# Cumulative sums of an attention's log weights: one fp32 product replaced by two products of split values

## The chip, the core and the metric

The kernel is one program on one core of a Trainium2 chip. The metric is the device time of one execution in microseconds, as the median of several runs. Beside it stands one profiled execution, whose trace has the start and the duration of every instruction on each engine: TensorE (PE, with its weight loads as PEld), VectorE (DVE), ScalarE (ACT), GpSimd (POOL) and the DMA queue of SyncE (SPq). All times below are in microseconds from the first instruction of that execution unless marked ns.

## The reference, cut to what matters

Two transformer blocks run one after the other on 256 tokens of 1024 features. The change is in the second block, in one of its three branches, a stick-breaking attention with 8 heads of 64 features:

```python
z = jnp.einsum("bhqd,bhkd->bhqk", q_blk, k[:, :, :ctx]) * scale
mask = k_pos[None, :] < q_pos[:, None]
log_1m_beta = jnp.where(mask, jax.nn.log_sigmoid(-z), 0.0)
cs = lax.cumsum(log_1m_beta, axis=3)
log_a = jax.nn.log_sigmoid(z) + (cs[..., -1:] - cs)
a = jnp.where(mask, jnp.exp(log_a), 0.0)
outs.append(jnp.einsum("bhqk,bhkd->bhqd", a, v[:, :, :ctx]))
```

The rest of the block around it is an input projection to 6656 columns, a gated spatial mixing (branch a), a 31-tap causal convolution (branch b), sigmoid gates for the three branches, an output projection, and a convolved feed-forward.

## The kernel before

Every large weight goes through the same line. SyncE loads a unit of up to 128x2048 values into one of four `raw` slots. ScalarE copies it to `w_hi` in the type fp32r (`high`, L516). VectorE writes `w_lo = raw - w_hi`, also fp32r (`low`, L866). TensorE then makes three fp32r products for each tile of it: high by high, high by low, low by high (L1361 to L1363). ScalarE and VectorE do this three blocks ahead of TensorE (`AHEAD`), and TensorE waits for `raw_used` of the block before it starts on it.

The stage with the change is `z_in`, the input projection: 26 blocks in the order of `Z_ORDER` (step s is block s). Every engine runs its own loop over the steps, in program order, and meets the others at semaphores. Into these steps the work on the branches is set by hand: `QK_STEP(p)` = 13 + 2p is where the scores of head pair p are made, `U_STEP(p)` = 15 + 2p where their log weights are, `AV_STEP(p)` = 17 + 2p where the values are weighted, for p = 0 to 3. `VLN_STEP` is 13, `SG_STEP` 14, `CV_MEAN_STEP` 22, `CV_VAR_STEP` 23.

For one pair of heads (keys on the partitions, 384 columns of queries a head) the attention goes like this. TensorE makes the scores in two PSUM banks (`scores`, L1666 and L1668). ScalarE computes log(1 + exp(-|z|)) in three passes into `sp_t` (`softplus_log`, L725 to L727). VectorE adds max(z, 0), which gives the softplus `sp` (`softplus`, L1194). GpSimd zeroes what the mask excludes (`mask`, L495). TensorE adds to the scores the product of a triangle of -1 (`neg_upper`) or a square of -1 (`neg_ones`) with `sp`: that is the cumulative sum over the keys (`log_weights`, L1677 to L1681; six fp32 products for a pair, of 256, 128 and 128 columns for each of two heads). VectorE clamps the result into `att` (`clamp`, L1203), ScalarE takes its exponential (`weights`, L731), GpSimd masks again, and TensorE multiplies by the values (`att_values`, L1695 and L1696).

Between these stand, on VectorE, the taps of the convolution (`conv`, L1186; a few in each step by the table `CONV_AT`), and at step 14 the eviction of the spatial mixing to `sgo` and its split to `br_a_hi` and `br_a_lo` (L1244 to L951). The spatial mixing has the PSUM bank pair 6 and 7, which the scores of pair 1 use next; so TensorE's `scores(1)` waits for `br_a` to reach 4, the last of these splits. `log_weights(p)` waits for `sp_masked`, the mask. The column means of the convolution (`cv_mean`, L1753, step 22) wait for the last of the 124 taps (`conv_step`).

Of the kernel before, what the change touches and what calls it, by code (L numbers as in the profile page):

```python
# [20 lines left out]
P = 128  # L21
T = 256
# [50 lines left out]
N_CONST = 10  # L73
# [3 lines left out]
VLN_STEP, SG_STEP = 13, 14  # L77
QK_STEP = lambda p: 13 + 2 * p
# [48 lines left out]
def build_program(nc, x_in, params, ada, ada_half, w, wm_t, sg_bias, sg_ln, out):  # L127
    f32, f32r = mybir.dt.float32, mybir.dt.float32r
    ALU, ACT = mybir.AluOpType, mybir.ActivationFunctionType
    ADD, SUB, MUL, MAX = ALU.add, ALU.subtract, ALU.mult, ALU.max  # L130
    ctx = ExitStack()
    with ctx:
        def sb(name, shape, dt=f32, c=ctx):
            return c.enter_context(nc.sbuf_tensor(name, shape, dt))

        def sem(name):
            return ctx.enter_context(nc.semaphore(name))
# [49 lines left out]
        with ExitStack() as c:  # L187
            br = {}
            for name in ("a", "c"):
                br[name] = [sb(f"br_{name}_{part}", [P, 4, T], f32r, c=c) for part in ("hi", "lo")]  # L190
            cacc = sb("cacc", [P, 4, T], c=c)
            vv = sb("vv", [P, 2, SG], c=c)
            head_ones = sb("head_ones", [P, P], c=c)
            neg_upper = sb("neg_upper", [P, P], c=c)
            neg_ones = sb("neg_ones", [P, P], c=c)
            bn = sb("bn", [P, 2, 8], c=c)
            vstd = sb("vstd", [P, 4], c=c)
            with ExitStack() as early:
                sig = sb("sig", [P, 2, T], c=early)
                sb("unused_gates_head", [P, 4, T], c=early)  # L200
                sgo = sb("sgo", [P, 4, T], c=early)
                vg = sb("vg", [P, 2, SG], c=early)
                wm = sb("wm", [P, HEADS, P], c=early)
                sgb = sb("sgb", [P, 4, P], c=early)
                sgln = sb("sgln", [P, 2, SG], c=early)
            gates = sb("gates", [P, 24, T], c=c)
            with ExitStack() as early:
                cpad = sb("cpad", [P, 4, T + CV_TAPS - 1], c=early)
                sp_t = sb("sp_t", [P, 2, 384], c=early)
            br["b"] = [sb(f"br_b_{part}", [P, 4, T], f32r, c=c) for part in ("hi", "lo")]  # L210
            with ExitStack() as late:
                mg_t = sb("mg_t", [P, 3, T], c=late)
            sp = sb("sp", [P, 2, 512], c=c)
            with ExitStack() as early:
                u_sb = sb("u_sb", [P, 4, T], c=early)
            att = sb("att", [P, 2, 512], c=c)
# [8 lines left out]
        ps = ctx.enter_context(nc.psum_tensor("ps", [P, 8, 2 * T], f32))  # L225
# [15 lines left out]
        const_set = sem("const_set")  # L241
# [61 lines left out]
        sp_log = sem("sp_log")  # L303
        sp_ready = sem("sp_ready")
        sp_masked = sem("sp_masked")
        loga_done = sem("loga_done")
        loga_low = sem("loga_low")
        att_exp = sem("att_exp")
# [198 lines left out]
        def _(act):  # L507
            e = act
# [210 lines left out]
            def softplus_log(p):  # L719
# [6 lines left out]
                ch.link(e.activation(sp_t[:, :, :], sp_t[:, :, :], ACT.Exp, scale=-1.0))  # L726
                e.activation(sp_t[:, :, :], sp_t[:, :, :], ACT.Ln, bias=1.0).then_inc(sp_log, 1)  # L727

            def weights(p):
                e.wait_ge(loga_low, p + 1)  # L730
                e.activation(att[:, :, 0:384], att[:, :, 0:384], ACT.Exp).then_inc(att_exp, 1)  # L731

            for s, kind in enumerate(Z_ORDER):
                g = FIRST["z_in"] + s
                high_at(g + AHEAD)
                bank = Z_FILL[s] % 2 if s in Z_FILL else None
                if s == CV_VAR_STEP:
                    for t in range(2):
                        e.wait_ge(cv_cent, 2 * t + 2)
                        square(SQ["cv"] + t, flat(cacc[:, 2 * t:2 * t + 2, :]))  # L740
# [117 lines left out]
        def _(dve):  # L858
# [329 lines left out]
            def softplus(p):  # L1188

                e.wait_ge(sp_log, p + 1)  # L1190
                if p:
# [2 lines left out]
                e.scalar_tensor_tensor(sp[:, :, 0:384], ps[:, zb:zb + 2, 0:384], 0.0, sp_t[:, :, :], MAX, ADD)\  # L1194
                 .then_inc(sp_ready, 1)

            def clamp(p):

                e.wait_ge(loga_done, p + 1)
                if p:  # L1200
                    e.wait_ge(att_done, p)
                zb = Z_BANKS[p % 2]
                e.tensor_scalar(att[:, :, 0:384], ps[:, zb:zb + 2, 0:384], 0.0, None, ALU.min).then_inc(loga_low, 1)  # L1203
# [4 lines left out]

            for s, kind in enumerate(Z_ORDER):
                g = FIRST["z_in"] + s  # L1210
                if s != SG_STEP:
                    ahead_at(g + AHEAD)
                bank = Z_FILL[s] % 2 if s in Z_FILL else None
# [141 lines left out]
        def _(pe):  # L1355
# [316 lines left out]
            def log_weights(p):  # L1672

                zb = Z_BANKS[p % 2]
                e.wait_ge(sp_masked, p + 1)
                for h in range(2):
                    e.matmul(ps[:, zb + h, 0:T], neg_upper[:, :], sp[:, h, 0:T], start=False, stop=True,  # L1677
                             skip_group_check=True)
                    e.matmul(ps[:, zb + h, P:T], neg_ones[:, :], sp[:, h, T:T + P], start=False, stop=True,
                             skip_group_check=True)  # L1680
                    mm = e.matmul(ps[:, zb + h, T:T + P], neg_upper[:, :], sp[:, h, T:T + P], start=False, stop=True,  # L1681
                                  skip_group_check=True)
                mm.then_inc(loga_done, 1)

            def att_values(p):
# [211 lines left out]
```

## Time and profile before

| | |
|---|---|
| runs | 766.95, 766.12, 766.15 us; median 766.15 us |
| profiled execution | 766.32 us, of which 764.6 us are the span from the first to the last instruction |
| PE busy | 749.6 us (98% of the span) |
| PEld busy | 696.9 us (91%) |
| DVE busy | 545.1 us (71%) |
| ACT busy | 360.3 us (47%) |
| POOL busy | 10.7 us (1%) |
| mean granted clock of TensorE | 0.998 of 2.4 GHz |

TensorE is busy nearly all the time; the other engines have gaps. The shares are means over nine stages. A matmul's duration in the trace is longer than what it takes of the engine's time, since matmuls overlap: what one costs is read from the distance between starts. One fp32 matmul of the program shows as two matmul records, one fp32r matmul as one.

### The profile page before, as it was taken

Reading aid. Unit: us, or ns where it says so; the run is one execution under the profiler, and the core shown is the slowest. Engines: PE = TensorE matmul, PEld = TensorE weight load, DVE = VectorE, ACT = ScalarE, POOL = GpSimd, SP = SyncE. Lnnn points to the kernel's source line nnn. Section 1 sums busy time; section 2 is a strip of 40 time slices with the busy share of each in tenths; the row PEclk is TensorE's granted clock in tenths of the full one; section 3 lists DMA queues with packets and bytes.
Section 4 is the critical chain, followed back from the end, with each engine's and each line's share of the span. In section 5 each row is a group of like instructions: output and inputs, shape, how many; then the busy total and the mean of one; then the engine's idle time right before and its main releaser. Section 6 shows DMA issues by size and latency. Waiting matters only on the chain.

```text
span 764.6 us, 13287 instructions
## 1 busy us (share of the span) xinstructions
PE 749.6 (98%) x5388; PEld 696.9 (91%) x5388; DVE 545.1 (71%) x770; ACT 360.3 (47%) x442; POOL 10.7 (1%) x27
## 2 busy tenths in 40 slices
PE   6999999999999999999999999999989999999998
PEld 5789955999998888899979999999989999999998
DVE  5677988856566743458899967769757888888441
ACT  4116332754553333475555366484546455554330
POOL 0000000000000000020000001000000000000000
PEclk9999999999999999999999999999999999999999
DMA  9999998364566964436445342437543544533640
GB/s 272 303 335 386 385 355 322 129 222 165 175 209 219 346 205 165 166 124 221 165 165 171 113 159 97 166 110 250 205 165 123 207 167 174 192 116 124 216 142 28
DMA packets 61728, 152.18 MB, mean 199 GB/s; under 512 B 2992, under 2 KB 42288, under 8 KB 51440
## 3 DMA queue, kind: packets, MB, share of 16 engines
q1 hardware_dynamic: 61312, 150.20, 57.3%
q0 software_dynamic: 368, 1.31, 0.5%
q8 instruction: 34, 0.56, 0.3%
q14 instruction: 14, 0.11, 0.0%
HBM read 150.45 MB, written 1.05 MB: 198 GB/s over the span
## 4 chain that ended last, share of the span: by engine, by line
PE 95%; SPq 3%; DMA 1%; ACT 1%; DVE 0%; issue 0%; DVEq 0%
PE ps L1363 21%; PE ps L1361 21%; PE ps L1362 21%; PE ps L1438 4%; PE ps L1518 4%; PE ps L1517 4%; PE ps L1516 4%; PE ps L1563 4%; SPq L390 2%; DMA keyed_odd<-in_w_sc_in 1%; PE ps L1652 1%; PE ps L1651 1%; PE ps L1650 1%; PE ps L1378 1%; PE ps L1501 1%; PE ps L1503 1%
## 5 line engine op out<-in xcount | busy, mean ns | idle before, releaser
L866 DVE TENSOR_TENSOR w_lo<-raw,w_hi 128x2048 fp32r<-128x2048 f32 (+2 forms) x116 | 246.2, 2124 | 94.2 <-ACT w_hi L516 93.9
L1361 PE MATMUL ps<-a_hi,w_hi 128*128 128x256 f32 x1072 | 305.2, 285 | 0.0
L1363 PE MATMUL ps<-a_hi,w_lo 128*128 128x256 f32 x1072 | 303.5, 283 | 0.0
L1362 PE MATMUL ps<-a_lo,w_hi 128*128 128x256 f32 x1072 | 301.1, 281 | 0.0
L516 ACT ACTIVATE w_hi<-raw 128x2048 fp32r<-128x2048 f32 (+2 forms) x116 | 205.8, 1778 | 105.5 <-PE ps L1518 50.3
L1362 PEld LDWEIGHTS ps<-a_lo,w_hi 128*128 128x128 f32 x1072 | 203.5, 190 | 0.6 <-issue 0.5
L1361 PEld LDWEIGHTS ps<-a_hi,w_hi 128*128 128x128 f32 x1072 | 201.7, 188 | 1.3 <-issue 0.6
L1363 PEld LDWEIGHTS ps<-a_hi,w_lo 128*128 128x128 f32 x1072 | 200.8, 187 | 0.0
L1516 PE MATMUL ps<-w_hi,hid_hi 128*128 128x512 f32 x128 | 50.9, 398 | 0.0
L1518 PE MATMUL ps<-w_hi,hid_lo 128*128 128x512 f32 x128 | 50.8, 397 | 0.0
L1517 PE MATMUL ps<-w_lo,hid_hi 128*128 128x512 f32 x128 | 50.8, 397 | 0.0
L842 ACT ACTIVATE up_u<-ps,par 128x256 f32<-128x256 f32 x44 | 22.5, 561 | 58.7 <-PE ps L1363 55.7
L1363 PE MATMUL ps<-up_hi,w_lo 128*128 128x256 f32 x176 | 49.8, 283 | 0.0
L1361 PE MATMUL ps<-up_hi,w_hi 128*128 128x256 f32 x176 | 49.8, 283 | 0.0
L1324 DVE SCALAR_TENSOR_TENSOR up_u<-ps,par,up_u 128x255 f32<-128x255 f32 (+1 forms) x88 | 38.4, 478 | 15.6 <-ACT up_u L842 13.4
L1362 PE MATMUL ps<-up_lo,w_hi 128*128 128x256 f32 x176 | 49.4, 280 | 0.0
L1186 DVE SCALAR_TENSOR_TENSOR cacc<-cpad,par,cacc 128x256 f32<-128x256 f32 x120 | 49.2, 480 | 0.0
L1362 PEld LDWEIGHTS ps<-up_lo,w_hi 128*128 128x128 f32 x176 | 33.5, 190 | 0.0
L1361 PEld LDWEIGHTS ps<-up_hi,w_hi 128*128 128x128 f32 x176 | 33.0, 188 | 0.0
L1363 PEld LDWEIGHTS ps<-up_hi,w_lo 128*128 128x128 f32 x176 | 33.0, 187 | 0.0
L1518 PEld LDWEIGHTS ps<-w_hi,hid_lo 128*128 128x128 f32 x128 | 24.1, 188 | 5.8
L1516 PEld LDWEIGHTS ps<-w_hi,hid_hi 128*128 128x128 f32 x128 | 24.1, 189 | 5.7
(242 smaller groups left out, 914.1 us busy)
## 6 DMA issues: line engine op xcount, KB each, us to landing
raw<-in_w_z_in SPq DMA_DIRECT2D x26, 1024.0 KB, 4.7
raw<-in_w_up SPq DMA_DIRECT2D x22, 1024.0 KB, 4.8
raw<-in_w_mlp_in SPq DMA_DIRECT2D x16, 1024.0 KB, 4.8
raw<-in_w_mlp_out SPq DMA_DIRECT2D x16, 1024.0 KB, 5.6
raw<-in_w_down SPq DMA_DIRECT2D x16, 704.0 KB, 4.1
raw<-in_ada SPq DMA_DIRECT2D x32, 256.0 KB, 6.2
raw<-in_ada_half SPq DMA_DIRECT2D x8, 1024.0 KB, 7.4
raw<-in_ada SPq DMA_DIRECT2D x8, 1024.0 KB, 7.1
```

The costliest lines, as they stand in the source:

```text
L516: e.activation(w_hi[:, slot, 0:words], raw[:, unit_slot, 0:words], ACT.Copy).then_inc(w_high, 1)
L866: e.tensor_tensor(w_lo[:, slot, 0:words], raw[:, unit_slot, 0:words], w_hi[:, slot, 0:words].bitcast(f32), SUB).then_inc(raw_used, 1)
L1186: e.scalar_tensor_tensor(cacc[:, i, :], src, wt, cacc[:, i, :], MUL, ADD).then_inc(conv_step, 1)
L1324: ins = e.scalar_tensor_tensor(dst, ps[:, b, h * T:(h + 1) * T - o], pdyn("up_w", it * 24 + (3 * (2 * b + h) + tap)), dst, MUL, ADD)
L1361: e.matmul(dst, w_hi[:, slot, cols], hi, start=start, stop=False, skip_group_check=skip)
L1362: e.matmul(dst, w_hi[:, slot, cols], lo, start=False, stop=False, skip_group_check=skip)
L1363: return e.matmul(dst, w_lo[:, slot, cols], hi, start=False, stop=stop, skip_group_check=skip)
L1438: mm = e.matmul(half(bank, h), lhs, y[:, k, :], start=opens, stop=k == DT - 1, skip_group_check=True)
L1516: e.matmul(dst, hi[:, tok], high_w, start=first, stop=False)
L1517: e.matmul(dst, hi[:, tok], low_w, start=False, stop=False)
L1518: return e.matmul(dst, lo[:, tok], high_w, start=False, stop=final)
L1563: mm = e.matmul(ps[:, 2 * c + h, :].rearrange("p (n q) -> p n q", n=4), sc_y[:, k, c * P:(c + 1) * P], by_feature[:, 4 * h:4 * h + 4, k, : ...
```

## The change

The softplus values are split, as the weights are: ScalarE copies masked `sp` to `sp_hi` in fp32r (`log_high`), VectorE writes `sp_lo = sp - sp_hi` in fp32r (`log_low`), both at the head of step `QK_STEP(p) + 1`. The two sign matrices are copied once to fp32r (`ones_r`, `upper_r`; -1 and 0 need no low part). `log_weights` then makes twelve fp32r products in place of six fp32 ones, and waits for `sp_low` in place of `sp_masked`. The fp32 sign matrices move into unused columns of `sp`; the new buffers lie where early ones have ended.

```diff
-            neg_upper = sb("neg_upper", [P, P], c=c)
-            neg_ones = sb("neg_ones", [P, P], c=c)
...
-                sb("unused_gates_head", [P, 4, T], c=early)
+                sb("unused_gates_head", [P, 3, T], c=early)
...
+                upper_r = sb("upper_r", [P, P], f32r, c=early)
+                ones_r = sb("ones_r", [P, P], f32r, c=early)
...
-                sp_t = sb("sp_t", [P, 2, 384], c=early)
+                with ExitStack() as log_part:
+                    sp_t = sb("sp_t", [P, 2, 384], c=log_part)
+                sp_hi = sb("sp_hi", [P, 2, 384], f32r, c=early)
...
             sp = sb("sp", [P, 2, 512], c=c)
+            neg_ones, neg_upper = sp[:, 0, 384:512], sp[:, 1, 384:512]
+            sp_lo = sb("sp_lo", [P, 2, 384], f32r, c=c)
...
+            def log_high(p):
+
+                e.wait_ge(sp_masked, p + 1)
+                if p:
+                    e.wait_ge(loga_done, p)
+                e.activation(sp_hi[:, :, :], sp[:, :, 0:384], ACT.Copy).then_inc(sp_high, 1)
...
                 high_at(g + AHEAD)
                 bank = Z_FILL[s] % 2 if s in Z_FILL else None
+                if s == VLN_STEP:
+                    e.wait_ge(const_set, N_CONST)
+                    e.activation(ones_r[:, :], neg_ones[:, :], ACT.Copy).then_inc(sign_ready, 1)
+                    e.activation(upper_r[:, :], neg_upper[:, :], ACT.Copy).then_inc(sign_ready, 1)
+                for p in range(4):
+                    if s == QK_STEP(p) + 1:
+                        log_high(p)
...
+            def log_low(p):
+
+                e.wait_ge(sp_high, p + 1)
+                e.tensor_tensor(sp_lo[:, :, :], sp[:, :, 0:384], sp_hi[:, :, :].bitcast(f32), SUB).then_inc(sp_low, 1)
...
                 g = FIRST["z_in"] + s
+                for p in range(4):
+                    if s == QK_STEP(p) + 1:
+                        log_low(p)
                 if s != SG_STEP:
                     ahead_at(g + AHEAD)
...
             def log_weights(p):
 
                 zb = Z_BANKS[p % 2]
-                e.wait_ge(sp_masked, p + 1)
-                for h in range(2):
-                    e.matmul(ps[:, zb + h, 0:T], neg_upper[:, :], sp[:, h, 0:T], start=False, stop=True,
-                             skip_group_check=True)
...
+                e.wait_ge(sign_ready, 2)
+                e.wait_ge(sp_low, p + 1)
+                for part in (sp_hi, sp_lo):
+                    for h in range(2):
+                        e.matmul(ps[:, zb + h, 0:T], upper_r[:, :], part[:, h, 0:T], start=False, stop=True,
+                                 skip_group_check=True)
+                        e.matmul(ps[:, zb + h, P:T], ones_r[:, :], part[:, h, T:T + P], start=False, stop=True,
+                                 skip_group_check=True)
+                        mm = e.matmul(ps[:, zb + h, T:T + P], upper_r[:, :], part[:, h, T:T + P], start=False, stop=True,
+                                      skip_group_check=True)
                 mm.then_inc(loga_done, 1)
```

Where the two new operations stand in their engines' order is best seen in the list of instructions. First VectorE in the kernel before, from the softplus of pair 0 (end of step 13) to the first eviction of step 14, whose last split is what `br_a` counts:

```order
L1186 SCALAR_TENSOR_TENSOR cacc<-cpad,par,cacc 128x256 [waits conv_step] x4
L1194 SCALAR_TENSOR_TENSOR sp<-ps,sp_t 128x2x384 [waits sp_log]
L1244 TENSOR_TENSOR sgo<-ps,sgb 128x128 [waits z_free_act,sg_done]
L1244 TENSOR_TENSOR sgo<-ps,sgb 128x128
L1248 TENSOR_TENSOR sgo<-sgo,u_sb 128x256 [waits dve_self]
L950 CAST br_a_hi<-sgo 128x256 [waits dve_self]
L951 TENSOR_TENSOR br_a_lo<-sgo,br_a_hi 128x256 [waits dve_self]
```

And the same place in the changed kernel:

```order
L1207 SCALAR_TENSOR_TENSOR cacc<-cpad,par,cacc 128x256 [waits conv_step] x4
L1215 SCALAR_TENSOR_TENSOR sp<-ps,sp_t 128x2x384 [waits sp_log]
L1221 TENSOR_TENSOR sp_lo<-sp,sp_hi 128x768 [waits sp_high]
L1273 TENSOR_TENSOR sgo<-ps,sgb 128x128 [waits z_free_act,sg_done]
L1273 TENSOR_TENSOR sgo<-ps,sgb 128x128
L1277 TENSOR_TENSOR sgo<-sgo,u_sb 128x256 [waits dve_self]
L971 CAST br_a_hi<-sgo 128x256 [waits dve_self]
```

The subtraction stands directly behind the softplus whose masked copy it needs, and ahead of all of step 14. For pairs 1 to 3 it stands the same way, directly behind the softplus, and ahead of the weights' low part and of the taps of its step.

ScalarE in the changed kernel, from the last pass of pair 0 (step 13) to step 15; before, the same rows stood there without the `sp_hi` one:

```order
L734 ACTIVATE sp_t<-sp_t 128x768 [waits act_self]
L523 ACTIVATE w_hi<-raw 128x2048 [waits w_used,raw_in1]
L741 ACTIVATE sp_hi<-sp 128x768 [waits sp_masked]
L803 ACTIVATE gates<-ps,par 128x256 [waits w_used]
L803 ACTIVATE gates<-ps,par 128x256
L523 ACTIVATE w_hi<-raw 128x2048 [waits w_used,raw_in2]
```

The copy to `sp_hi` comes behind a weight's copy and ahead of the gates. The copies of the sign matrices stand in step 13, between a weight's copy and `u_sb`.

## Rows read from the trace of the kernel before

**Rows 1.** The page's first part: busy time, share, instructions.

```profile
PE 749.6 (98%) x5388; PEld 696.9 (91%) x5388; DVE 545.1 (71%) x770; ACT 360.3 (47%) x442; POOL 10.7 (1%) x27
```

**Rows 2.** Windows: stretch, length, then each engine's busy time, granted clock.

```profile
405.00:500.00 95.00, 95.00 (x780) 90.95 (x780) 77.67 (x132) 52.03 (x67) 5.10 (x8) 1.00 0.38 133
```

**Rows 3.** Timeline of PE: start, union of durations, instructions with their record count.

```profile
431.23 0.59 PE L1677 MATMUL ps<-sp,neg_upper 128*128 128x256 f32 x2
431.66 0.39 PE L1679 MATMUL ps<-sp,neg_ones 128*128 128x128 f32 x2
431.89 0.39 PE L1681 MATMUL ps<-sp,neg_upper 128*128 128x128 f32 x2
...
433.08 0.71 PE L1666 MATMUL ps<-y 64*128 64x256 f32 x4
...
446.45 0.70 PE L1677 MATMUL ps<-sp,neg_upper 128*128 128x256 f32 x2
...
448.41 0.71 PE L1666 MATMUL ps<-y 64*128 64x256 f32 x4
...
477.12 0.70 PE L1677 MATMUL ps<-sp,neg_upper 128*128 128x256 f32 x2
...
484.74 1.89 PE L1753 MATMUL ps<-cacc,ones 128*128 128x256 f32 x8
```

**Rows 4.** Timeline of DVE: start, duration; in brackets the idle time before.

```profile
424.93 0.95 DVE L1194 SCALAR_TENSOR_TENSOR sp<-ps,sp_t 128x768 f32<-128x768 f32 x1
425.80 0.48 DVE L1244 TENSOR_TENSOR sgo<-ps,sgb 128x128 f32<-128x128 f32 x2
...
432.23 0.42 DVE L951 TENSOR_TENSOR br_a_lo<-sgo,br_a_hi 128x256 fp32r<-128x256 f32 x1
...
444.07 0.96 DVE L1194 SCALAR_TENSOR_TENSOR sp<-ps,sp_t 128x768 f32<-128x768 f32 x1 [3.37 <-ACT sp_t L727]
445.87 2.29 DVE L866 TENSOR_TENSOR w_lo<-raw,w_hi 128x2048 fp32r<-128x2048 f32 x1 [0.84 <-ACT w_hi L516]
...
481.65 2.07 DVE L1186 SCALAR_TENSOR_TENSOR cacc<-cpad,par,cacc 128x256 f32<-128x256 f32 x5
```

**Rows 5.** Timeline of POOL, the masks of `sp` for pairs 0, 1, 3.

```profile
426.01 0.64 POOL L495 TENSOR_SCALAR_AFFINE_SELECT sp<-sp 128x512 f32<-128x512 f32 x1 [92.80 <-DVE sp L1194]
...
445.16 0.64 POOL L495 TENSOR_SCALAR_AFFINE_SELECT sp<-sp 128x512 f32<-128x512 f32 x1 [2.82 <-DVE sp L1194]
...
474.54 0.64 POOL L495 TENSOR_SCALAR_AFFINE_SELECT sp<-sp 128x512 f32<-128x512 f32 x1 [2.81 <-DVE sp L1194]
```

**Rows 6.** Timeline of ACT.

```profile
416.76 0.60 ACT L767 ACTIVATE u_sb<-ps 128x512 f32<-128x512 f32 x1 [3.36 <-PE ps L1363]
...
443.19 0.85 ACT L727 ACTIVATE sp_t<-sp_t 128x768 f32<-128x768 f32 x1
443.94 1.90 ACT L516 ACTIVATE w_hi<-raw 128x2048 fp32r<-128x2048 f32 x1
```

**Rows 7.** Timeline of PE: two fp32r products of 256 columns, neighbours.

```profile
434.28 0.28 PE L1363 MATMUL ps<-a_hi,w_lo 128*128 128x256 f32 x1
434.40 0.28 PE L1361 MATMUL ps<-a_hi,w_hi 128*128 128x256 f32 x1
```

**Rows 8.** The weight loads of one line whose products have one column.

```profile
L1419 PEld LDWEIGHTS ps<-silu_c,raw x16: 191/192/193, 11.7 to 13.4; 128*128 128x128 f32 x16
```

**Rows 9.** Groups by line from 405 to 500, weight loads: busy, mean ns.

```profile
L1362 PEld LDWEIGHTS ps<-a_lo,w_hi 128*128 128x128 f32 x207 | 39.1, 189 | 0.1
...
L1677 PEld LDWEIGHTS ps<-sp,neg_upper 128*128 128x128 f32 x16 | 2.4, 190 | 0.5 <-issue 0.5
```

**Rows 10.** Timeline of PE behind its longest wait in the up stage.

```profile
570.14 0.55 PE L1501 MATMUL ps<-a_hi,w_hi 128*128 128x256 f32 x1 [2.14 <-ACT a_hi L561]
```

**Rows 11.** Windows around that wait; the third number from the end is the clock.

```profile
566.20:569.90 3.70, 1.16 (x5) 0.68 (x4) 0.84 (x3) 1.83 (x4) 0.00 (x0) 1.00 0.31 131
569.90:573.30 3.40, 3.16 (x15) 3.19 (x16) 3.40 (x11) 3.40 (x9) 0.00 (x0) 0.50 0.00 0
```

More of the change, by code:

```diff
@@ L305, in build_program @@
         sp_masked = sem("sp_masked")
+        sign_ready = sem("sign_ready")
+        sp_high = sem("sp_high")
+        sp_low = sem("sp_low")
         loga_done = sem("loga_done")
@@ L1674, in log_weights @@
                 zb = Z_BANKS[p % 2]
-                e.wait_ge(sp_masked, p + 1)
-                for h in range(2):
-                    e.matmul(ps[:, zb + h, 0:T], neg_upper[:, :], sp[:, h, 0:T], start=False, stop=True,
-                             skip_group_check=True)
[L1679 to L1682, printed above, removed]
+                e.wait_ge(sign_ready, 2)
[8 more added lines that the diff above has]
+                                      skip_group_check=True)
                 mm.then_inc(loga_done, 1)
```

## The prediction

> **What bounds the kernel now.** I read the page's first part, then windows, then the timelines of the engines between 405 and 500 us, where all four head pairs lie. TensorE is busy 98% of the span [rows 1], and in the stage of the change 95.00 of 95.00 us, at full granted clock [rows 2]. So TensorE sets the end, and two things can move it: what its own instructions cost, and a wait that did not exist. The second needs the distance between a result and its use, which no share shows. I looked for it in three places.
>
> First place, `scores(1)`. TensorE starts it at 433.08, right behind `log_weights(0)` [rows 3]. It waits for the last split of branch a, which ends at 432.23 + 0.42 = 432.65 [rows 4]. Room: 0.43 us.
>
> Second place, `log_weights(p)`. For pair 1 the mask ends at 445.16 + 0.64 = 445.80 [rows 5], TensorE uses it at 446.45 [rows 3]: 0.65 us of room. For pair 3 it is 475.18 against 477.12: 1.94 us. For pair 0 it is 426.65 against 431.23.
>
> Third place, `cv_mean`, at 484.74 [rows 3]. The last taps end at 481.65 + 2.07 = 483.72 [rows 4]: 1.02 us of room.
>
> VectorE has idle time, but little that it could give away here. Before the softplus of a pair it waits for ScalarE's passes [rows 4], those wait for the previous pair's exponential, that for VectorE's clamp. It is a ring: clamp, exponential, three passes, softplus, weights and taps, next clamp. What is put into the ring makes each turn longer, and nothing in it waits for TensorE.
>
> **The change, part by part.**
>
> *TensorE's products.* For pair 0 the six fp32 products and the switch to the scores take 433.08 - 431.23 = 1.85 us: 0.43 for 256 columns, 0.23 for 128 (431.66 to 431.89) [rows 3]. For pair 1 it is 448.41 - 446.45 = 1.96; the 0.11 more stands behind `att_values`. An fp32r product of 256 columns takes 0.12 [rows 7]. One of 128 columns with 128 columns of weights isn't in the trace. Lower bound: half of 0.12, 0.06. Next row: sixteen fp32 records of one moving column start from 11.7 to 13.4, 0.113 each, so the weight load holds the distance there [rows 8]. Upper bound: the fp32 price, 0.23, if the short form gains nothing. I take 0.113, since a weight load in fp32r lasts 189 ns and in fp32 190 [rows 9]. Twelve products are then 4 x 0.12 + 8 x 0.113 = 1.38, against 2 x 0.43 + 4 x 0.225 = 1.76: 0.38 less for a pair (0.8 less at the lower bound, 0.56 more at the upper).
>
> The Trainium skill (TensorE: Matmul & The Clock Gate, Weight-path perf modes) says that a fast weight load is on when there are 128 weights and the input type is not FP32. If fp32r counted as such a type, its load would be shorter than fp32's; the trace has 189 and 190 ns, so it does not agree for this type. By the page the products would go to the lower bound, 0.8 us less for a pair in place of 0.38, and the waits below would swallow it.
>
> *ScalarE, signs.* Two copies of 128x128 in step 13, ahead of `u_sb`, before which ScalarE waits 3.36 us [rows 6]. Each costs less than the 0.60 of the four times wider `u_sb`. Hidden. Without that cover they would cost under 1.2 us, once.
>
> *ScalarE and VectorE, pair 0.* Now the copy waits for the mask (426.65), takes 0.85 like a pass of the same 768 columns [rows 6], and the subtraction takes 0.96 like the softplus of 768 columns [rows 4]. From GpSimd to ScalarE I allow 0.1 (VectorE to GpSimd shows 426.01 - 425.88 = 0.13 [rows 4, 5]), from ScalarE to VectorE 0.03 (444.04 to 444.07 [rows 4, 6]). So: copy 426.75 to 427.6, subtraction 427.63 to 428.6. Next instructions start about 0.1 before the end of the one ahead, so `sgo` starts at 428.5 in place of 425.80: **VectorE is 2.7 us late**. Queued behind the subtraction is the whole of step 14, and who waits for it is TensorE: `br_a` is complete at 435.35, `scores(1)` starts at 435.4 in place of 433.08. TensorE is 2.3 us late, and the 0.38 us of cheaper products has gone into the wait. ScalarE's gates of step 14 are late too; the bank that they free is needed behind `scores(1)`, so after 435.4, and comes at about 428.4.
>
> *Pair 1.* Before, the weight's copy ended at 443.94 + 1.90 = 445.84, and VectorE went on with the low part at 445.87 [rows 4, 6]. Now `sp_hi` follows: 445.9 to 446.75, the subtraction 446.78 to 447.75, the low part at 447.67. **1.8 us more per turn**, all of it serial. With the 2.7 from before, `sp_low` is there at 450.45. TensorE arrives at 446.45 + 2.3 = 448.77 and starts at 450.5: 4.05 late, after a wait of 1.7. Cheaper products give back 0.38 + 0.1 (the switch lies in the wait): 3.6 late.
>
> *Pairs 2 and 3.* Pair 2 goes the same way: VectorE 6.3 us late behind it. For pair 3 the mask ends at 475.18 + 6.3 = 481.48, `sp_low` at 483.4. TensorE would be there at about 481.7 (pair 2 makes it 4.5 late, by the same steps) and starts at 483.45, 6.3 late, 5.85 after the products.
>
> *The mean of the convolution.* VectorE is late by 2.7 + 3 x 1.8 = 8.1, so the taps end at 491.8. TensorE would arrive at 484.74 + 5.85 = 490.6; it starts at 491.87, **7.1 us late**. From here on I count no further wait. The squares for the variance follow VectorE, which is then 8.1 late against TensorE's 7.1; if they had no room for that 1.0, it would come on top. The weights for the blocks are ahead: VectorE's low part is for a block three later, some 17 us of TensorE's work, against at most 8.1 us.
>
> *Sum.* 764.6 + 7.1 = 771.7 for the span. Against the profiled execution's own time that is 766.32 + 7.1 = 773.4; the median of the runs is 0.17 less, so 773.3. The price of the products hardly enters: at the upper bound they are 0.94 us dearer than I took for pair 3, and the wait for the taps holds 1.3.
>
> The bounds of the hand-overs: with nothing from GpSimd to ScalarE, pair 0 gives 2.6 and a turn 1.75 (the weight's copy ends last there), the end 6.8 later. With 0.3 it is 2.9 and 2.0: 7.9 later. If the copy to `sp_hi` costs 0.70 instead of 0.85, 0.6 less; if the subtraction runs 0.2 dearer, 0.8 more.
>
> **The rivals.**
>
> *The products at 0.23 (they don't do what the change says).* They cost 4 x 0.12 + 8 x 0.23 = 2.3 in place of 1.76. By the waits above the end stays at 773.3, at most 773.6. Nothing in the trace speaks against it, since no short fp32r product is in it. Chance 0.33.
>
> *The clock falls in the new waits.* In the up stage TensorE waits 2.14 us, in a window in which it is busy 1.16 of 3.70, and in the 3.40 us after it the granted clock is 0.50 [rows 10, 11]. The new waits are 1.2 to 2.7 us long, but each stands alone in dense work. One fall costs 3.4 x 0.5 = 1.7 us of work. After one of the first waits the next swallows it; after the last ones 0.4 to 1.7 stay. Time: 773.7 to 775.0, I take 774.8. Chance 0.12. The same fall in the up stage could also be missed once everything is shifted: 1.5 less, which is in the range.
>
> *TensorE keeps the pace* (the other side). If the ring had slack enough, only the products would count: 4 x -0.38 = -1.5, so 764.6; at the lower bound of the products 4 x -0.8, so 763.0. It decides if the copy and the subtraction together take less than 0.43 us behind the mask's own 0.64 at step 14 and less than 0.65 for pair 1. By the rows they take 1.8. Chance 0.03; that such slack is there for a part and the sum lands within 0.2%, another 0.02.
>
> The 763.0 is also where the Trainium skill's fast weight load (TensorE: Matmul & The Clock Gate, Weight-path perf modes) would lead if TensorE kept the pace.
>
> **How the numbers follow.** The forecast (waits in the ring, products at 0.113) has 0.50, the rival with the same end 0.33, the clock 0.12, the two others 0.05. Predicted 773.3. The cases that agree on the ring span 772.0 to 774.9 by their bounds; I widen to 771.4 and 775.4 for a clock fall won or lost and for the 1.0 at the squares. What a measurement can tell from no change is about 0.2%, 1.5 us: slower 0.95, same 0.02, faster 0.03.
>
> **What would show it.** In the changed trace: TensorE waits before `scores(1)` for VectorE's last `br_a_lo`, before `log_weights` of pairs 1 to 3 for the subtraction, and before `cv_mean` for the taps, 8.5 us together; a distance of 0.11 or of 0.23 between short products; VectorE idle 1.7 us before the first subtraction. It would be wrong if the ring had room that I missed, if the mask, copy and subtraction overlap, or if the clock falls more than once.

## The result, and the profile after

The changed kernel takes 772.86 us (median of 4 runs, 771.79 to 774.55), the kernel before on the same chip 766.55 us (766.12 to 767.48): a ratio of 1.0084, 95% interval 1.0069 to 1.0100. It is slower, by 6.3 us. The profiled execution took 774.55 us, with a span of 772.8 us.

The page's first part of the changed kernel, to be read against [rows 1]:

```profile
PE 752.4 (97%) x5388; PEld 699.8 (91%) x5388; DVE 548.2 (71%) x774; ACT 364.3 (47%) x448; POOL 10.7 (1%) x27
```

No share moved by more than a point: VectorE has 3.1 us more work, ScalarE 4.0, and TensorE is still at 97%. The loss can't be seen there. The windows can show it. Here is the changed kernel over the stretch of [rows 2], then from the start of `scores(0)` to the start of `cv_mean` (the stage), and from there to the end; the third figure from the end of a row is the granted clock:

```profile
405.00:500.00 95.00, 89.46 (x730) 86.20 (x728) 76.43 (x123) 50.68 (x65) 5.11 (x8) 0.96 0.35 121
...
416.71:491.82 75.11, 69.57 (x569) 66.97 (x569) 58.57 (x93) 38.48 (x49) 4.47 (x7) 0.95 0.34 117
491.82:772.80 280.98, 275.48 (x2250) 273.34 (x2248) 196.65 (x291) 138.90 (x162) 0.64 (x1) 0.99 0.46 158
```

And the same two stretches of the kernel before:

```profile
416.65:484.74 68.09, 68.09 (x569) 65.07 (x569) 55.73 (x90) 35.22 (x46) 4.46 (x7) 1.00 0.37 132
484.74:764.60 279.86, 274.33 (x2250) 272.19 (x2248) 196.26 (x290) 138.77 (x162) 0.64 (x1) 0.99 0.45 158
```

Of the 8.2 us between the two spans, 7.0 lie in the stage, where TensorE was busy throughout and now isn't, 1.1 behind it, and 0.1 ahead. What ends the new idle time is in the list of TensorE's waits of the changed kernel (sum, times, longest):

```profile
PE ps L1708 <- DVE sp_lo L1221: 2.9, 2, 1.7
PE ps L1695 <- DVE br_a_lo L972: 2.5, 1, 2.5
PE ps L1530 <- ACT a_hi L568: 2.1, 1, 2.1
```

The third row was there before [rows 10]; the first two are new, and both are for VectorE. VectorE's timeline of the changed kernel shows why it is late, against [rows 4]:

```profile
424.99 0.95 DVE L1215 SCALAR_TENSOR_TENSOR sp<-ps,sp_t 128x768 f32<-128x768 f32 x1
427.62 0.96 DVE L1221 TENSOR_TENSOR sp_lo<-sp,sp_hi 128x768 fp32r<-128x768 f32 x1 [1.68 <-ACT sp_hi L741]
428.50 0.48 DVE L1273 TENSOR_TENSOR sgo<-ps,sgb 128x128 f32<-128x128 f32 x2
...
434.74 0.43 DVE L972 TENSOR_TENSOR br_a_lo<-sgo,br_a_hi 128x256 fp32r<-128x256 f32 x1
...
446.57 0.96 DVE L1215 SCALAR_TENSOR_TENSOR sp<-ps,sp_t 128x768 f32<-128x768 f32 x1 [3.37 <-ACT sp_t L734]
449.21 0.96 DVE L1221 TENSOR_TENSOR sp_lo<-sp,sp_hi 128x768 fp32r<-128x768 f32 x1 [1.68 <-ACT sp_hi L741]
450.09 2.29 DVE L887 TENSOR_TENSOR w_lo<-raw,w_hi 128x2048 fp32r<-128x2048 f32 x1
...
462.77 0.96 DVE L1215 SCALAR_TENSOR_TENSOR sp<-ps,sp_t 128x768 f32<-128x768 f32 x1 [2.58 <-ACT sp_t L734]
...
489.26 2.06 DVE L1207 SCALAR_TENSOR_TENSOR cacc<-cpad,par,cacc 128x256 f32<-128x256 f32 x5
```

Each subtraction stands behind 1.68 us in which VectorE does nothing, since mask and copy run on other engines in that time; its own 0.96 comes on top. `sgo` begins at 428.50 in place of 425.80, 2.7 later, and the last `br_a_lo` ends at 435.17 in place of 432.65. The last taps end at 491.32 in place of 483.72: VectorE is 7.6 us late. GpSimd's mask and ScalarE's copy in the same trace:

```profile
426.07 0.64 POOL L502 TENSOR_SCALAR_AFFINE_SELECT sp<-sp 128x512 f32<-128x512 f32 x1 [92.70 <-DVE sp L1215]
```
```profile
426.74 0.85 ACT L741 ACTIVATE sp_hi<-sp 128x768 fp32r<-128x768 f32 x1 [2.94 <-POOL sp L502]
...
446.45 1.90 ACT L523 ACTIVATE w_hi<-raw 128x2048 fp32r<-128x2048 f32 x1
448.34 0.84 ACT L741 ACTIVATE sp_hi<-sp 128x768 fp32r<-128x768 f32 x1
```

The mask ends at 426.71, the copy starts at 426.74: 0.03 from GpSimd to ScalarE. For pair 1 the copy follows right at the end of the weight's copy, 448.35. TensorE's timeline of the changed kernel has the products and two of the waits:

```profile
431.58 0.34 PE L1708 MATMUL ps<-sp_hi,upper_r 128*128 128x256 f32 x1
431.76 0.22 PE L1710 MATMUL ps<-sp_hi,ones_r 128*128 128x128 f32 x1
431.81 0.28 PE L1712 MATMUL ps<-sp_hi,upper_r 128*128 128x128 f32 x1
431.93 0.34 PE L1708 MATMUL ps<-sp_lo,upper_r 128*128 128x256 f32 x1
...
435.31 0.71 PE L1695 MATMUL ps<-y 64*128 64x256 f32 x4 [2.53 <-DVE br_a_lo L972]
...
436.47 0.41 PE L1391 MATMUL ps<-a_lo,w_hi 128*128 128x256 f32 x1
436.68 0.41 PE L1392 MATMUL ps<-a_hi,w_lo 128*128 128x256 f32 x1
...
450.32 0.36 PE L1708 MATMUL ps<-sp_hi,upper_r 128*128 128x256 f32 x1
...
483.10 0.36 PE L1708 MATMUL ps<-sp_hi,upper_r 128*128 128x256 f32 x1 [1.67 <-DVE sp_lo L1221]
```

A head's three products for one part take 431.93 - 431.58 = 0.35 us, so twelve take 1.4. The products of 256 columns at 436.47 and 436.68 stand 0.21 apart, where [rows 7] have 0.12: TensorE's clock has fallen behind the first wait. The windows of the changed kernel around the two waits, and in the up stage:

```profile
433.00:436.20 3.20, 0.89 (x9) 0.80 (x9) 3.06 (x8) 0.00 (x0) 0.00 (x0) 1.00 0.00 0
436.20:439.70 3.50, 3.50 (x18) 3.50 (x18) 3.50 (x4) 0.00 (x0) 0.00 (x0) 0.51 0.36 87
480.80:484.00 3.20, 1.53 (x16) 1.23 (x13) 2.00 (x2) 3.20 (x5) 0.29 (x1) 1.00 0.00 0
484.00:487.50 3.50, 3.50 (x18) 3.50 (x18) 3.50 (x7) 1.23 (x3) 0.00 (x0) 0.51 0.33 65
...
576.00:583.00 7.00, 5.79 (x27) 5.82 (x28) 6.87 (x17) 5.02 (x10) 0.00 (x0) 0.52 0.00 0
```

Behind each of these two waits TensorE ran some 3.4 us at the half level, 1.2 GHz (0.51 in the windows of 3.50). In the up stage the half level lasts 7 us here, where the kernel before had 3.4 [rows 11]. Behind the fall at 484.0 the taps, ready at 491.32, were no longer what `cv_mean` waited for: it follows its own predecessors, at 491.82.

### The profile page after: what moved, and what is told of

The parts are those of the page before. It is cut to its first block, busy times and chain, and to the rows that moved or that the text cites. A ratio compares the mean times of both kernels' runs of the same rounds, so it can differ in the third digit from the quotient of the medians.

```text
span 772.8 us, 13304 instructions
## 1 busy us (share of the span) xinstructions
PE 752.4 (97%) x5388; PEld 699.8 (91%) x5388; DVE 548.2 (71%) x774; ACT 364.3 (47%) x448; POOL 10.7 (1%) x27
## 3 DMA queue, kind: packets, MB, share of 16 engines
q0 software_dynamic: 368, 1.31, 0.5%
## 4 chain that ended last, share of the span: by engine, by line
PE 86%; DVE 6%; ACT 3%; SPq 3%; issue 1%; DMA 1%; POOL 0%; DVEq 0%; ACTq 0%; POOLq 0%
PE ps L1392 19%; PE ps L1391 19%; PE ps L1390 19%; PE ps L1467 4%; PE ps L1547 4%; PE ps L1546 4%; PE ps L1545 4%; PE ps L1592 4%; SPq L397 2%; DVE w_lo L887 2%; DVE cacc L1207 2%; DMA keyed_odd<-in_w_sc_in 1%; PE ps L1680 1%; PE ps L1681 1%; PE ps L1679 1%
```

## Experiments

Theory: the loss is VectorE's lateness in the ring, handed to TensorE at `scores(1)`, at `log_weights` and at `cv_mean`; the products themselves gain. Rivals: the products are what costs; the falls of the clock are what costs. Each profile is cut as above, at the start of `scores(0)` and at the start of `cv_mean`. All numbers are us; "half" counts the stretches of about 3.4 us at half clock in the stage and behind it (7 us on end are two). The waits stand in order of time: the first of a row is at `scores(1)`, the next are at `log_weights` of pairs 1 to 3, and "mean" is the one at `cv_mean`.

| kernel | stage | behind it | half | TensorE's waits in the stage |
|---|---|---|---|---|
| before | 68.09 | 279.86 | 0, 1 | none |
| changed | 75.11 | 280.98 | 2, 2 | 2.53, 0.1, 1.28, 1.67 |
| changed, again | 74.63 | 278.57 | 1, 0 | 2.53, 0.14, 1.26, 1.63, mean 0.92 |
| split only | 74.64 | 278.53 | 0, 0 | 2.10, 1.56, 0.83, 1.22, mean 0.53 |
| products only | 67.10 | 280.03 | 0, 1 | 0.09, mean 0.44 |
| low part of pair 0 late | 73.49 | 281.10 | 1, 2 | 0.95, 1.56, 1.26, 1.67 |
| clamp first | 70.47 | 279.70 | 1, 1 | 2.53 |
| waits filled | 74.66 | 280.03 | 0, 1 | 0.16, 1.65, 1.27, 0.05, mean 0.99 |
| before, clamp first | 68.08 | 279.72 | 0, 1 | none |
| low part on GpSimd | 69.51 | 279.73 | 0, 1 | 1.31, 1.75 |
| ring filled | 67.35 | 281.08 | 0, 2 | 0.95 |
| softplus(0) first | 67.50 | 279.97 | 0, 1 | 0.47, 0.58 |
| taps later | 66.88 | 279.96 | 0, 1 | 0.47 |

### The split alone

The changed kernel with the six fp32 products back; it still waits for `sp_low`, whose values it does not use.

```diff
                 e.wait_ge(sp_low, p + 1)
-                for part in (sp_hi, sp_lo):
-                    for h in range(2):
-                        e.matmul(ps[:, zb + h, 0:T], upper_r[:, :], part[:, h, 0:T], start=False, stop=True,
...
+                for h in range(2):
+                    e.matmul(ps[:, zb + h, 0:T], neg_upper[:, :], sp[:, h, 0:T], start=False, stop=True,
```

> Change: the changed kernel with its copy to sp_hi, its subtraction to sp_lo and all its waits, but log_weights makes the six fp32 products of the kernel before. Theory W (the copy and subtraction lengthen the ring of VectorE and ScalarE, and TensorE waits for it): the products lie in front of waits, so the time stays that of the changed kernel within 0.7 us, about 6.4 to 7 above the kernel before; TensorE still waits before scores(1), log_weights of pairs 1 to 3, but less, as it gets there later. Theory P (the short fp32r products themselves are what costs): back to the kernel before, +0. If costs simply add up with products 0.38 cheaper a pair: +7.9.

773.57 us (771.92 to 774.48) against 766.37: 1.0098 (1.0085 to 1.0112). The windows of this kernel, stage and the part behind it:

```profile
416.93:491.57 74.64, 68.41 (x569) 65.04 (x568) 58.10 (x93) 38.48 (x49) 4.48 (x7) 1.00 0.33 115
491.57:770.10 278.53, 273.02 (x2248) 270.87 (x2248) 196.98 (x291) 138.92 (x162) 0.64 (x1) 1.00 0.47 160
```

And its waits:

```profile
PE ps L1707 <- DVE sp_lo L1221: 3.6, 3, 1.6
...
PE ps L1695 <- DVE br_a_lo L972: 2.1, 1, 2.1
...
PE ps L1783 <- DVE cacc L1207: 0.5, 1, 0.5
```

The stage is 6.55 longer than before at full clock throughout, with all five waits: VectorE's lateness alone makes the loss. If costs simply added up, the dearer products would have made the time 7.9 longer; it is 7.2. Dearer products only shorten the waits in front of `cv_mean`, whose start is set by the taps.

### The products alone

The kernel before with twelve fp32r products of the same rounded `sp`. It leaves out the split; the sums come out doubled.

```diff
-            sp = sb("sp", [P, 2, 512], c=c)
+            sp = sb("sp", [P, 2, 512], f32r, c=c)
...
+                for part in (sp, sp):
```

> Change: the kernel before with the sign matrices copied to fp32r and twelve fp32r products, all of them of one tile that the softplus writes as fp32r; there is no split (so high part used twice, the sums are doubled: it leaves out the split) and log_weights waits for the mask as before. Theory W: nothing waits, TensorE sets the pace, 4 x -0.38 and up to 0.1 more for each: -1.5 to -1.9 us against the kernel before. Theory P: +6.

766.01 us (764.44 to 767.09, 11 runs) against 766.37: 0.9997 (0.9987 to 1.0006). The stage is 1.0 shorter, and TensorE's timeline of this kernel shows what stopped it:

```profile
484.57 1.78 PE L1762 MATMUL ps<-cacc,ones 128*128 128x256 f32 x7 [0.44 <-DVE cacc L1193]
```

The products gave at least 1.5 (1.0 and the two waits, 0.53), and 1.7 where the taps hold nothing up (with the ring filled, below: 68.09 + 0.95 - 67.35). The taps had just 1.02 of room, so the rest became a wait. Not even the cheaper products by themselves have their full worth in this order: the forecast of 1.5 to 1.9 was missed.

### The low part of pair 0 behind the first tile of the spatial mixing, and the clamp ahead of the taps

Each is one move on VectorE in the changed kernel. The first:

```diff
-                for p in range(4):
+                for p in range(1, 4):
                     if s == QK_STEP(p) + 1:
                         log_low(p)
...
+                        if t == 0:
+                            log_low(0)
```

> Change: the changed kernel, only pair 0's subtraction moved behind the first of the four tiles of the spatial mixing, so VectorE has work while mask and copy run. Theory W: VectorE's wait of 1.68 us disappears, scores(1) is late by about 0.9 in place of 2.5, and as the ring keeps the whole lead, TensorE's later starts all move 1.7 earlier: 1.7 us below the changed kernel, +4.7 against before. If only the later turns of the ring count (slack takes up pair 0): 0 below the changed kernel. Theory K (clock falls make most of it): below by up to 3, since the longest wait goes.

772.12 us (771.34 to 774.06): 1.0075 (1.0061 to 1.0088). `scores(1)` waits 0.95 in place of 2.53, and the stage is 1.6 shorter, as expected. The three waits for the subtractions are what they are in the changed kernel where no fall goes before them (1.56, 1.26, 1.67; 1.65 and 1.27 with the waits filled). The time is 5.75 above the kernel before, where 4.7 was forecast; the profile had two stretches at half clock behind the stage. The second move:

```diff
-                if s in CONV_AT:
-                    first = sum(n for step, n in CONV_AT.items() if step < s)
-                    conv(first, first + CONV_AT[s])
                 for p in range(4):
...
                         clamp(p)
+                if s in CONV_AT:
+                    first = sum(n for step, n in CONV_AT.items() if step < s)
+                    conv(first, first + CONV_AT[s])
```

> Change: the changed kernel, only that VectorE clamps att ahead of the step's taps and not behind them (steps 15, 17, 19, 21), so the taps fill its wait for ScalarE's passes. Theory W: a turn of the ring gets about 2.06 shorter (16.2 to 14.1), under TensorE's 14.9 for the same stretch; no wait at log_weights 1 to 3 nor at the taps; only the wait at scores(1) stays, 2.3, less 3 x 0.38: +1.2 against before, up to +2.9 if the clock falls behind that wait. If the ring isn't what TensorE waits for: as the changed kernel, +6.4.

769.59 us (768.38 to 771.42): 1.0049 (1.0033 to 1.0064). It takes the taps, some 2 us, out of the chain clamp, exponential, passes, softplus. All waits but the first, 2.53 at `scores(1)`, are gone.

The stage is 2.4 longer than before. The wait gives 2.53 and the cheaper products take 1.7 back, so the fall of the clock behind the wait cost about 1.5. That is less than half of its 3.4 us: a product takes 0.21 there in place of 0.12. The time, 3.2 above the kernel before, is a little over the 2.9 that was expected with a fall. The same move in the kernel before is the control:

> Control: the kernel before, only with the clamp ahead of the taps. Theory W: TensorE waits for nothing there before and after, so the time is that of the kernel before within 0.2 us, and scores(0) to the mean stays 68.1 us. If the shorter ring by itself gave e4 its gain: about -3.

766.57 us (11 runs): 0.9998 (0.9987 to 1.0008), and a stage of 68.08: where TensorE waits for nothing, a shorter ring gives nothing.

### The waits filled

Products that no one uses stand ahead of two waits, so that TensorE is busy in them.

```diff
+            def fill(n):
+                e.wait_ge(rstd_ready, STATN["cv"])
+                for _ in range(n):
+                    e.matmul(ps[:, STAT, 0:P], head_ones[:, :], head_ones[:, :], start=True, stop=True)
...
                 if p == 1:
+                    fill(10)
                     e.wait_ge(br_a, 4)
...
+                if p == 3:
+                    fill(6)
                 e.wait_ge(sp_low, p + 1)
```

> Change: the changed kernel, and TensorE makes ten small fp32 products (128x128, 0.225 us each, into the unused statistics bank, never read) just ahead of its wait in scores(1), and six ahead of the wait in log_weights(3); they lie in waits of 2.5 and 1.7 us. Theory W alone: they cost nothing and give nothing, +6.4 against before. Theory K (in most runs of the changed kernel the granted clock falls behind these waits, and that costs up to about 0.5 us at the mean of the convolution): no fall to 0.50 between 430 and 500 us in the profile, the distance from scores(0) to the mean of the convolution is set by the last taps, 74.7 us in place of 75.1, and the median falls by 0.3 to 0.6 us, more if the phase of the later fall matters.

773.68 us (773.14 to 774.48): 1.0091 (1.0076 to 1.0106). Its windows, the first two where the changed kernel has its first wait and fall, the third over the stage:

```profile
433.00:436.20 3.20, 3.04 (x28) 2.70 (x27) 3.06 (x8) 0.00 (x0) 0.00 (x0) 1.00 0.02 5
436.20:439.70 3.50, 3.50 (x30) 3.50 (x31) 3.50 (x4) 0.00 (x0) 0.00 (x0) 1.00 0.29 70
```
```profile
416.71:491.37 74.66, 70.54 (x602) 67.49 (x601) 58.12 (x93) 38.48 (x49) 4.48 (x7) 1.00 0.32 115
```

The falls in the stage are gone, and the time is no shorter. That speaks against the clock as the cause, and the table says why: with no fall in the stage the taps set its end, at 74.66. The changed kernel once more:

> The changed kernel once more, for a comparison on one chip and for how much of its time is chance. Theory W: +6.4 against before, scores(0) to the mean 74.7 to 75.1 us. Theory K: the spread of its runs is that of the number of clock falls; the run with none behind the waits lies 0.5 us and more below the others.

773.33 us (771.62 to 773.94) against 767.17: 1.0083 (1.0070 to 1.0097). Its stage is 74.63 although the clock fell behind `scores(1)`: the next wait, for `sp_lo` of pair 1, is 0.14 here and 1.65 where nothing fell. So what the fall cost, 1.5 by this difference, went into it. Only the fall behind the last `log_weights`, in the first profile of the changed kernel, came through, with 75.11 - 74.65 = 0.5, the part of its 1.5 that is more than the wait for the taps. Without one at that place the taps held `cv_mean`:

```profile
492.13 1.13 PE L1784 MATMUL ps<-cacc,ones 128*128 128x256 f32 x4 [0.92 <-DVE cacc L1207]
```

### The subtraction on GpSimd

The clamp ahead of the taps, and GpSimd makes `sp_lo` in VectorE's place.

```diff
                 mask(sp, sp_masked, p + 1)
+                e.wait_ge(sp_high, p + 1)
+                e.tensor_tensor(sp_lo[:, :, :], sp[:, :, 0:384], sp_hi[:, :, :].bitcast(f32), SUB).then_inc(sp_low, 1)
```

> Change: the changed kernel with the subtraction to sp_lo made by GpSimd right behind its mask, not by VectorE, and the clamp ahead of the taps. Theory W: VectorE's order has nothing new in it, so scores(1) starts as in the kernel before, without a wait; the copy and a subtraction of 1 to 2.5 us on GpSimd end before log_weights(0) (room 4.6 us) and, as the clamp's move gives 2.06 us per turn, before log_weights of the others. TensorE then keeps the pace: 4 x -0.38 and 3 x -0.1 at most, -1.5 to -1.9 against before, scores(0) to the mean 66.3 us. If GpSimd takes over 3 us or slows VectorE down: a wait at log_weights(1) of 1 us or more.

769.53 us (767.52 to 772.07): 1.0041 (1.0027 to 1.0054), where 1.5 to 1.9 us below the kernel before was forecast: missed. The profiled execution is the fastest of the eight, and no fall is in its stage, which is 1.4 longer than before. Of the runs the two at a mean granted clock of 0.998 took 767.52 and 767.67, the three at 0.993 770.95 to 772.07: in the median falls of the clock are counted along with the waits. The tile `sp_lo` of this kernel (least, median and most ns):

```profile
L510 POOL TENSOR_TENSOR sp_lo<-sp,sp_hi x4: 1848/3022/3057, 427.6 to 474.5; 128x768 fp32r<-128x768 f32 x4
```

Beside it VectorE is slower too, as its timeline shows:

```profile
427.53 0.48 DVE L1267 TENSOR_TENSOR sgo<-ps,sgb 128x128 f32<-128x128 f32 x2
428.05 1.67 DVE L1271 TENSOR_TENSOR sgo<-sgo,u_sb 128x256 f32<-128x256 f32 x1
...
430.93 0.43 DVE L1271 TENSOR_TENSOR sgo<-sgo,u_sb 128x256 f32<-128x256 f32 x1
...
445.03 2.29 DVE L889 TENSOR_TENSOR w_lo<-raw,w_hi 128x2048 fp32r<-128x2048 f32 x1 [0.85 <-ACT w_hi L525]
```

And GpSimd's:

```profile
427.58 1.85 POOL L510 TENSOR_TENSOR sp_lo<-sp,sp_hi 128x768 fp32r<-128x768 f32 x1 [1.03 <-ACT sp_hi L743]
...
445.98 3.00 POOL L510 TENSOR_TENSOR sp_lo<-sp,sp_hi 128x768 fp32r<-128x768 f32 x1 [1.03 <-ACT sp_hi L743]
```

The same instruction takes 0.43 alone and 1.67 while GpSimd subtracts from 427.58 to 429.43. The Trainium skill (SBUF — State Buffer, SBUF: two separate sides) says that a VectorE instruction with two inputs in SBUF and a GpSimd instruction that reads SBUF exclude each other for the whole instruction. The trace agrees: VectorE's instruction is 1.67 - 0.43 = 1.24 longer, GpSimd had 1.38 still to go when it began, and the eviction with one input in PSUM beside it kept its 0.48. It agrees the other way round too: GpSimd's 3.00 of pair 1 began at 445.98, while VectorE's low part, with two inputs in SBUF, ran to 447.32, and it is 1.15 longer than the 1.85 of pair 0. Two waits of TensorE stay: 1.31 at `scores(1)`, which the slowed multiplication by `u_sb` makes, and 1.75 at `log_weights(1)`, which GpSimd's 3 us make.

### The ring filled, and two more orders of it

The subtractions stay on VectorE, but what VectorE waits through is filled: four taps ahead of each of the last three, the first tile of the spatial mixing ahead of pair 0's, and the clamp ahead of the taps.

```diff
+                for p in range(1, 4):
                     if s == QK_STEP(p) + 1:
+                        conv(taps_done(s), taps_done(s) + 4)
                         log_low(p)
...
+                        if t == 0:
+                            log_low(0)
...
+                if s in CONV_AT:
+                    early = 4 if s in (16, 18, 20) else 0
+                    conv(taps_done(s) + early, taps_done(s) + CONV_AT[s])
```

> Change: the changed kernel with its subtraction still on VectorE, but no wait of VectorE left bare: pair 0's behind the first tile of the spatial mixing, the others' behind four taps of their step, and the clamp ahead of the taps. Theory W: a turn of the ring is 12.6 us, TensorE's 14.9; only scores(1) waits, 0.9 us. scores(0) to the mean: 68.1 + 0.6 - 3 x 0.46 = 67.3 us, -0.8 against before. If VectorE's added 0.96 us a turn is by itself what TensorE waits for: +3 or more.

765.97 us (764.08 to 768.02, 11 runs) against 766.4: 0.9989 (0.9977 to 1.0000). The stage came out at the forecast 67.3, the time 0.4 below the kernel before, where 0.8 was forecast. VectorE's timeline of this kernel at pair 1:

```profile
443.86 0.96 DVE L1215 SCALAR_TENSOR_TENSOR sp<-ps,sp_t 128x768 f32<-128x768 f32 x1 [1.01 <-ACT sp_t L734]
444.73 2.04 DVE L1207 SCALAR_TENSOR_TENSOR cacc<-cpad,par,cacc 128x256 f32<-128x256 f32 x4
446.70 0.94 DVE L1224 TENSOR_TENSOR sp_lo<-sp,sp_hi 128x768 fp32r<-128x768 f32 x1
```

The taps stand where the 1.68 us stood, and the subtraction waits for nothing. With the split in place and VectorE's waits filled, the stage is shorter than before the change. This kernel has every copy, subtraction, new buffer and semaphore of the changed one: in this order none of them costs TensorE more than the 0.95 at `scores(1)`, which the products outweigh. Next, `softplus(0)` moves ahead of the taps of step 13, whose number becomes 2, with 4 in step 14:

```diff
-CONV_AT = {**{s: 7 for s in range(2, 8)}, **{s: 8 for s in range(8, 13)}, 13: 4, 14: 2, **{s: 5 for s in range(15, 22)}, 18: 6}
+CONV_AT = {**{s: 7 for s in range(2, 8)}, **{s: 8 for s in range(8, 13)}, 13: 2, 14: 4, **{s: 5 for s in range(15, 22)}, 18: 6}
...
+                if s == QK_STEP(0):
+                    softplus(0)
                 if s in CONV_AT:
```

> Change: e8, and in step 13 the softplus of pair 0 ahead of the taps, two of which move to step 14. Theory W: mask and copy of pair 0 end earlier, and the spatial mixing's eviction starts when TensorE has it ready, 0.3 us earlier than before; scores(1) waits about 0.5 in place of 0.95 us. scores(0) to the mean of the convolution 67.0 us (kernel before 68.1, e8 67.35), time 1.1 us below the kernel before. If scores(1) does not wait for br_a alone: as e8.

766.04 us (764.34 to 767.26, 11 runs) against 767.17: 0.9987 (0.9978 to 0.9996). `scores(1)` waits only 0.47, as expected, but the taps moved to step 14 made VectorE late for pair 1, a new wait of 0.58, and the stage came out at 67.50 in place of 67.0. Last, step 14 keeps its 2 taps and step 16 has 7:

```diff
-CONV_AT = {**{s: 7 for s in range(2, 8)}, **{s: 8 for s in range(8, 13)}, 13: 2, 14: 4, **{s: 5 for s in range(15, 22)}, 18: 6}
+CONV_AT = {**{s: 7 for s in range(2, 8)}, **{s: 8 for s in range(8, 13)}, 13: 2, 14: 2, **{s: 5 for s in range(15, 22)}, 16: 7, 18: 6}
```

> Change: e9, only that two taps lie in step 16 and not in step 14, where they stood between pair 0 and the clamp. Theory W: in e9 they made log_weights(1) wait 0.58 us; moved, VectorE reaches the clamp 0.8 us earlier and that wait goes, scores(1) keeps its 0.47. scores(0) to the mean 66.9 us in place of e9's 67.5, time 1.2 to 1.7 us below the kernel before. If the wait at log_weights(1) comes from ScalarE's or GpSimd's part of the chain: as e9.

765.29 us (764.82 to 767.15, 11 runs) against 766.43: 0.9985 (0.9974 to 0.9996). The windows of this kernel over stage and rest:

```profile
416.56:483.44 66.88, 66.41 (x569) 63.92 (x569) 63.26 (x96) 41.30 (x51) 7.33 (x8) 1.00 0.38 137
483.44:763.40 279.96, 274.43 (x2250) 272.27 (x2248) 194.01 (x288) 136.39 (x160) 0.00 (x0) 0.99 0.46 157
```

The stage is 1.2 us shorter than before the change, with one wait left, of 0.47, as forecast; the time is 1.1 below the kernel before. This version has a lower median than both kernels, by 0.15% and by about 1%; the first margin is below the 0.2% taken as what a measurement can tell, though its interval leaves 1 out.

## Why the prediction was right, by its own steps

**The sign of it, and the three places.** All held. TensorE waits at `scores(1)` for the last `br_a_lo`, before `log_weights` for the subtraction, and, where no fall comes just ahead of it, at `cv_mean` for the taps. The split alone gives the whole loss; the products alone give none. The waits add up to 5.5 in the first profile and 6.5 in the second, forecast 8.5: at 1.5 for each fall in the stage, the falls took most of the difference, since TensorE was slow in that time and did not wait.

**The products at 0.113.** Forecast 1.38 for twelve, measured 4 x 0.35 = 1.4. The rival with 0.23 is out. So is the lower bound of 0.06 as a mean, though single short ones start 0.05 behind their neighbour (431.76 to 431.81): the one ahead of it, or behind it, then takes the more. At full clock loads of `upper_r` last 186 to 192 ns, against 189 and 190 in [rows 9], so no shorter to speak of. That the price hardly enters the sum was also right: stages of 74.64 and 74.63 with fp32 and with fp32r products. The copies of the two sign matrices were hidden as forecast: 0.30 us each, from 413.36 on, and `u_sb` starts at 416.82 in place of 416.76, later by the same 0.06 as `scores(0)`.

**Pair 0.** Copy and subtraction stood within 0.03 of their forecast times. `scores(1)` was at 435.31, forecast 435.4.

**A turn at 1.8.** It is 1.7. From the softplus of pair 1 to the weight's low part VectorE takes 450.09 - 446.57 = 3.52, where it took 445.87 - 444.07 = 1.80 [rows 4]: 1.72 more, since ScalarE's copy begins at the very end of the weight's copy and instructions begin 0.1 before the end of the one ahead. The softplus of pairs 1 and 2 are 16.20 apart, 14.49 before. At the end VectorE is 7.6 late, forecast 8.1, because the second softplus was only 2.5 late (446.57 against 444.07), not 2.7, and three turns were 0.1 shorter each. `sp_low` of pair 1 was there at 450.17 (450.45), the last `log_weights` began at 483.10 (483.45).

**The end at +7.1.** The stage grew by 7.0 in the first profile, but by 6.55 in the three profiles in which the taps set its end (split only, waits filled, changed again). That is the size of the error: 0.5, the sum of the shorter turns. In the first profile a fall of the clock put back the 0.5, so the number agrees by an accident there. Of the medians, 6.3 and 6.2 above the kernel before, the forecast 7.1 was 0.8 to 0.9 too high.

**The clock.** The prediction gave 0.12 to a fall in the new waits and priced it at what the next wait doesn't swallow, 0.4 to 1.7. In the profiled execution two falls came, the first swallowed, the second worth 0.5. It was right as a mechanism, too unlikely, and priced a little high: a fall costs 1.5 us of work and not 3.4 x 0.5 = 1.7. The falls in the stage don't make the loss: the split alone and the filled waits lose as much, with none there in their profiles, and three of the four runs with filled waits had a mean granted clock of 0.998. But falls weigh on single runs. Of the nine runs of the changed kernel the three at 0.996 to 0.998 took 771.62 to 772.50, the six at 0.991 to 0.993 took 772.84 to 774.55. Where the clock fell in the runs that weren't profiled isn't known.

**What it took for granted: nothing behind the stage.** No new wait came there: TensorE is idle 5.50 us behind `cv_mean` in the changed kernel, 5.53 before. But the part behind `cv_mean` has 278.53 or 278.57 us with no half clock, 279.7 to 280.0 with one stretch of it, 281.0 to 281.1 with two, in thirteen profiles of twelve kernels. This is no part of the change: the kernel with the ring filled had two, the kernel before one, the changed kernel two and none. On average the first stretch adds 1.3 us to an execution and the second 1.2, each about a fifth of the effect. Why the up stage falls into one or the other was not tried, and stays open. The part ahead varies too: `scores(0)` starts anywhere from 416.56 to 418.00, at 416.71 and at 417.50 in the two profiles of the changed kernel. What also stays open is the spread of the medians: four comparisons whose profiles have the same stage within 0.5 (changed twice, split only, waits filled) gave 6.3, 6.2, 7.2 and 7.3 us over before, and so don't rank these kernels.

## What to carry to other kernels

An operation put on an engine with much idle time costs the whole hand-over (here mask 0.64, copy 0.85, subtraction 0.96; 2.7 at pair 0, and 1.7 at the others, where VectorE waited for a weight's copy before the change too), if the engine stands in a ring and the operation waits in program order: look for what is queued behind it, and put work that is ready into the wait, as the four taps were. Measure the room between result and use at each place where the bound engine could start to wait, since it caps a gain as well (1.0 of 1.5 to 1.7 for the products alone). Cut the span at two fixed instructions, so that a part which varies by itself is not counted for the change.

## What the runs showed of the hardware

Behind a wait of 2.53 us TensorE ran 3.4 us at half clock in every profile that had such a wait; behind 2.10 (split only) it did not. Behind 1.67 us it did in two profiles; behind 1.63, 1.65 and 1.75 it did not in three others. What such a stretch cost was about 1.5 us of work. A GpSimd subtraction of 128x768 values took 1.85 to 3.06 us, where VectorE needs 0.96, and a VectorE instruction with both inputs in SBUF took 1.67 beside it in place of 0.43.
